# First unit in halves, scalings one head ahead, and the mixer's norm factor on its products

## The reference

```python
h = h + recurrent_block(rmsnorm(h, a_norm), ...)   # u = x @ w_in; conv; gates; scan; @ w_out
h = h + sqrelu_mlp(rmsnorm(h, mlp_norm[0]), w_up[0], w_down[0])
k, v = shared_kv(h, ...)
h = h + chunk_band_attention(rmsnorm(q), k, v, rel_bias) @ b_w_o      # 16 heads
h = h + sqrelu_mlp(rmsnorm(h, mlp_norm[1]), w_up[1], w_down[1])
# second block, on the same h and on mem (256 x 1024)
p = rmsnorm(h, norm_mix_pre) @ w_in_2      # q,k,v of 3 attentions and 3 gates, 5888 columns
h = h + rmsnorm((sum over b of sigmoid(gate_b) * (attention_b @ w_branch_b)) @ w_out_2, ...)
h = h + rmsnorm((gelu(conv(u_gate)) * conv(u_val)) @ w_ffn_down_2, ...)   # conv over tokens
```

## Time and profile before

| | |
|---|---|
| profiled execution, its own time | 1075.28 us |
| its span, first to last instruction | 1073.5 us |
| median of the three timed runs | 1074.75 us |
| PE busy | 1032.0 us, 96% of the span |
| DVE, ACT, POOL busy | 662.0, 556.9, 85.8 us |
| mean granted TensorE clock | 0.990 |
| from HBM | 178.48 MB |

### The profile page before, as it was taken

The page is one execution under the profiler, slowest core; times in us unless marked ns, Lnnn a source line. Parts: engine busy times, 40 slices in busy tenths (PEclk is TensorE's granted clock), DMA queues, the critical chain, the costliest instruction groups (busy, mean ns, idle before and its releaser), DMA issues. The chain is left out here.

```text
span 1073.5 us, 16449 instructions
## 1 busy us (share of the span) xinstructions
PE 1032.0 (96%) x6698; PEld 927.5 (86%) x6698; DVE 662.0 (62%) x950; ACT 556.9 (52%) x817; POOL 85.8 (8%) x109
## 2 busy tenths in 40 slices
PE   5989999999999989999999989999999989999997
PEld 5888899999987755798999979988899879999997
DVE  5769665555557665565555554455655658878775
ACT  6598454444446464454444454455644446655552
POOL 3510010000002210030000000000001600000000
PEclk9989999999999999999999989999999999999999
DMA  9545586555536331475555537543333534655531
GB/s 312 189 137 164 189 302 208 178 184 185 196 118 218 135 118 40 158 238 193 192 186 171 193 101 214 169 146 102 98 137 137 198 117 160 232 170 185 195 118 40
DMA packets 120307, 180.41 MB, mean 168 GB/s; under 512 B 3145, under 2 KB 93609, under 8 KB 120249
## 3 DMA queue, kind: packets, MB, share of 16 engines
q1 hardware_dynamic: 118435, 174.16, 49.3%
q0 software_dynamic: 1696, 5.39, 1.5%
q10 hardware_dynamic: 118, 0.05, 0.0%
HBM read 178.48 MB, written 1.10 MB: 167 GB/s over the span
## 5 line engine op out<-in xcount | busy, mean ns | idle before, releaser
L1037 PE MATMUL PS<-XA,whi 128*128 128x256 f32 x2544 | 468.0, 286 | 4.6 <-DVE XA L1610 3.2
L1559 DVE TENSOR_TENSOR wlo<-raw,whi 128x2048 fp32r<-128x2048 f32 x155 | 356.6, 2305 | 172.3 <-ACT whi L611 172.3
L1037 PEld LDWEIGHTS PS<-XA,whi 128*128 128x128 f32 x2544 | 402.9, 193 | 14.2 <-issue 10.6
L611 ACT ACTIVATE whi<-raw 128x2048 fp32r<-128x2048 f32 x155 | 295.7, 1910 | 138.6 <-PE PS L1082 103.6
L1037 PE MATMUL PS<-XA,wlo 128*128 128x256 f32 x1272 | 361.7, 284 | 0.0
L1037 PEld LDWEIGHTS PS<-XA,wlo 128*128 128x128 f32 x1272 | 245.9, 193 | 0.0
L1082 PE MATMUL PS<-whi,XB 128*128 128x512 f32 x736 | 209.0, 391 | 0.0
L1082 PEld LDWEIGHTS PS<-whi,XB 128*128 128x128 f32 x736 | 135.6, 188 | 26.6 <-issue 0.5
L1082 PE MATMUL PS<-wlo,XB 128*128 128x512 f32 x368 | 117.5, 390 | 0.0
L1082 PEld LDWEIGHTS PS<-wlo,XB 128*128 128x128 f32 x368 | 69.1, 188 | 14.6
L787 ACT ACTIVATE arena<-PS 128x256 f32<-128x256 f32 x64 | 24.2, 383 | 96.2 <-PE PS L1037 95.7
(11 more groups left out here) (221 smaller groups left out, 1108.7 us busy)
## 6 DMA issues: line engine op xcount, KB each, us to landing
raw<-in_w_up SPq DMA_DIRECT2D x32, 1024.0 KB, 5.4
raw<-in_w_down SPq DMA_DIRECT2D x32, 1024.0 KB, 5.0
raw<-in_w_ffn_up SPq DMA_DIRECT2D x22, 1024.0 KB, 5.0
raw<-in_w_in SPq DMA_DIRECT2D x21, 1024.0 KB, 5.2
raw<-in_w_ffn_down SPq DMA_DIRECT2D x11, 1024.0 KB, 4.9
raw<-in_a_w_in SPq DMA_DIRECT2D x8, 1024.0 KB, 8.3
raw<-in_w_kv SPq DMA_DIRECT2D x8, 1024.0 KB, 5.0
raw<-in_w_mem_kv SPq DMA_DIRECT2D x4, 1024.0 KB, 5.1
```

The lines of the kernel that those rows point to most:

```text
L611: act.activation(whi[:, s, :], raw[:, s, :], ACT.Copy).then_inc(s_hi, 1)
L1037: ins = pe.matmul(PS[:, bank_of(g), 0:T], w[:, k, P * m:P * m + P], X[:, k0 + k, part, :], start=(i == 0 and part == 0 and w is hi), stop= ...
L1559: dve.tensor_tensor(wlo[:, s, :], raw[:, s, :], whi[:, s, :].bitcast(F32), ALU.subtract).then_inc(s_lo, 1)
```

## The change

- **Start.** `res` is loaded in two token halves and unit 0 in two halves of k. The 18 loads of small vectors are issued by SP (7) and ACT (11) instead of POOL (5), SP (7) and ACT (6). PE first runs 18 products of `ident` with itself, and 4 more behind the transposes (`keep_warm`). The vector rows are transposed between the two token halves. ACT copies the gains; the other vectors are copied by DVE later. Unit 0 is multiplied with k outermost. Its split is made in two halves on ACT and DVE, the second half on DVE behind four of the `XA` parts. Unit 1 is split on ACT in two halves among the `XA` copies.
- **Recurrent part.** ACT's wait for `s_ew` moves from behind `conv_hi(0)` to ahead of `gate_out(0)`.
- **Sixteen heads.** DVE scales the probabilities of H + 1 where it scaled those of H, behind the row maxima of H + 2; its split halves come one head later. ACT takes the exponentials of H + 2 ahead of the split half. The last split is at head 13 instead of 14.
- **Mixer's norm.** The second MLP's last product is lifted. `first_up` multiplies unit `U_QKV`. Squares are taken behind the `XA` copies, POOL's roots go to `dsc`. In the middle of unit `U_QKV + 1` PE multiplies `dsc` into a row (2 products, bank 7), and ACT copies it to `rstd_row`.
- **Mixer.** DVE evacuates 17 groups with a multiplication by `rstd_row`, followed by its split of unit u + 3; the two value results are scaled by `dsc`. In `gates` DVE multiplies each of the 24 groups by `rstd_row` into SBUF, behind its split; ACT's tanh reads that and stands behind `probs_out`.

The core of the diff:

```diff
@@ ACT, start and recurrent part
-            squares(SQ_NORM[0], res, lambda i: act.wait_ge(s_x, 16))
-            split(0)
-            norm_hi(0, [(XA, R_ANORM)])
-            split(1)
+            squares(SQ_NORM[0], res, lambda i: act.wait_ge(s_x[i // 2], 16))
+            for h, done in enumerate((s_hi0, s_hi)):
+                act.wait_ge(s_landed[0] if h else s_w0, 16)
+                at = slice(UNIT // 2 * h, UNIT // 2 * h + UNIT // 2)
+                act.activation(whi[:, 0, at], raw[:, 0, at], ACT.Copy).then_inc(done, 1)
...
             conv_hi(0)
 
-            act.wait_ge(s_ew, 32)
             rec_unit(2)
...
             conv_hi(3)
+
+            act.wait_ge(s_ew, 32)
             gate_out(0)
@@ DVE, start
+            for h, (ready, done) in enumerate(((s_hi0, s_lo0), (s_hi, s_lo))):
+                dve.wait_ge(ready, 1)
+                at = slice(UNIT // 2 * h, UNIT // 2 * h + UNIT // 2)
+                dve.tensor_tensor(wlo[:, 0, at], raw[:, 0, at], whi[:, 0, at].bitcast(F32), ALU.subtract).then_inc(done, 1)
...
+                for k in range(4 * h, 4 * h + 4):
+                    dve.wait_ge(s_xhi, NORM_HI[0] + k + 1)
...
@@ DVE, sixteen heads
             row_max(1)
+            norm_probs(0)
             for H in range(16):
-                norm_probs(H)
                 if H + 2 < 16:
                     row_max(H + 2)
+                if H + 1 < 16:
+                    norm_probs(H + 1)
...
                 for part in range(2):
-                    if H - part in SPLIT_AT:
-                        split(SPLIT_AT[H - part] + LEAD, part=part)
+                    if H - 1 - part in SPLIT_AT:
+                        split(SPLIT_AT[H - 1 - part] + LEAD, part=part)
@@ PE, mixer's norm
-            norm_T(5)
-            for i in range(2):
-                unit_a(U_QKV + i, G_QMB + 2 * i, xready=NORM_HI[5] if i == 0 else None)
+            first_up(U_QKV, G_QMB, 5, lambda: res_T(1, A_MLP1, 4))
+            have(U_QKV + 1)
+            group(G_QMB + 2, (U_QKV + 1) % SLOTS, 0, W8, KT, XA)
+            pe.wait_ge(s_rstd, ROOTS[SQ_NORM[5]] + TT)
+            for t in range(TT):
+                ins = pe.matmul(PS[:, 7, P * t:P * t + P], dsc[:, DS_MIX + t:DS_MIX + t + 1].to_broadcast([P, P]),
+                                ident[:], start=(t == 0), stop=(t == 1), skip_group_check=True)
+            ins.then_inc(s_bc, 1)
+            group(G_QMB + 3, (U_QKV + 1) % SLOTS, 1, W8, KT, XA)
@@ DVE, mixer
+            def rows_out(u, g, dsts, scale=1.0):
+
+                for m, dst in enumerate(dsts):
+                    dve.wait_ge(s_step, BEFORE(u) + m + 1)
+                    dve.scalar_tensor_tensor(dst, PS[:, bank_of(g + m), 0:T], scale, rstd_row[:], ALU.mult, ALU.mult)\
+                       .then_inc(s_evac, 1)
+                if u > U_QKV:
+                    split(u + LEAD)
...
                 if k % 2 == 0:
                     split(U_G2[b] + k // 2 + LEAD)
+                dve.wait_ge(s_step, BEFORE(U_G2[b]) + k + 1)
+                dve.tensor_tensor(g_br[b][:, k, :], PS[:, bank_of(G_G2[b] + k), 0:T], rstd_row[:], ALU.mult)\
+                   .then_inc(s_evac, 1)
@@ ACT, mixer
-                evac(G_G2[b] + k, BEFORE(U_G2[b]) + k + 1, g_br[b][:, k, :], ACT.Tanh, 0.5)
                 if H <= last:
                     probs_out(H)
+                act.wait_ge(s_evac, G_G2[b] + k + 1)
+                act.activation(g_br[b][:, k, :], g_br[b][:, k, :], ACT.Tanh, scale=0.5).then_inc(s_tanh, 1)
```

More of the change, by code:

```diff
@@ L298, in bass_blocks @@
         s_ident = sem("identity")
[L299 to L300 removed]
+        s_small, s_tables = sem("small_loads"), sem("bias_table_loads")
+        s_x = [sem(f"x_loaded{t}") for t in range(TT)]
+        s_w0 = sem("first_unit_half_landed")
+        s_hi0, s_lo0, s_gain = sem("first_unit_half_hi"), sem("first_unit_half_lo"), sem("norm_gains")
         s_mem = sem("mem_loaded")
@@ L446, in load @@
                 dst = raw[:, slot, :].rearrange("p (k n) -> p k n", k=w_units[u].shape[1])
+                if u == 0:
+                    for h in range(2):
+                        sp.dma_start(dst[:, 4 * h:4 * h + 4, :], w_units[u][:, 4 * h:4 * h + 4, :])\
+                          .then_inc(s_landed[slot] if h else s_w0, 16)
+                    return
                 if u in U_SWQ:
@@ L915, in _ @@
             mlp(1)
-            norm(5, res, [(XA, R_MIX)], added(A_MLP1))
-            two = lambda v, i: [v[:, 2 * i + m, :] for m in range(2)]
-            for i in range(2):
-                unit_a(U_QKV + i, G_QMB + 2 * i, two(qT_mb, i), scale=0.125)
-            for i in range(2):
-                unit_a(U_QKV + 2 + i, G_KMB + 2 * i, two(kT_mb, i))
-            for i in range(2):
-                unit_b(U_QKV + 4 + i)
-            for i in range(2):
-                unit_a(U_QKV + 6 + i, G_QSW + 2 * i, two(qT_sw, i), scale=0.125)
-            unit_a(U_QKV + 8, G_KSW, [kT_sw])
-            for i in range(2):
-                unit_a(U_QKV + 9 + i, G_QME + 2 * i, two(qT_me, i), scale=float(P) ** -0.5)
+            lift_hi(5, [(XA, R_MIX)], U_MLP1 + MLP_UNITS - 1)
+            squares_res(SQ_NORM[5])
+            unit_b(U_QKV)
+            unit_b(U_QKV + 1)
+            act.wait_ge(s_bc, 1)
+            act.activation(rstd_row[:], PS[:, 7, 0:T], ACT.Copy).then_inc(s_row, 1)
+            for i in range(2, 11):
+                unit_b(U_QKV + i)
             def gates(b, k, H, last):
@@ L1881, in _ @@
             mlp(1)
-            dve.wait_ge(s_rstd, ROOTS[SQ_NORM[4]] + TT)
-            add_out(A_MLP1, U_MLP1 + MLP_UNITS - 1, DS_MLP1)
-            norm(5, res, [(XA, R_MIX)], late=U_MLP1 + MLP_UNITS - 1 + LEAD)
-            for i in range(6):
-                split(U_QKV + i + LEAD)
-            dve.wait_ge(s_step, AFTER[U_QKV + 5])
-            dve.tensor_copy(v_mb, PS[:, 6:8, :]).then_inc(s_bev, 1)
-            for i in range(6, 9):
-                split(U_QKV + i + LEAD)
-            dve.wait_ge(s_step, AFTER[U_QKV + 8])
@@ L1894, in _ @@
-            dve.tensor_copy(v_sw, PS[:, 5, 0:T].rearrange("p (t n) -> p t n", t=TT)).then_inc(s_bev, 1)
-            for i in range(9, 11):
-                split(U_QKV + i + LEAD)
+            add_lift(A_MLP1, U_MLP1 + MLP_UNITS - 1, 5, [(XA, R_MIX)], U_MLP1 + MLP_UNITS - 1 + LEAD, DS_MLP1)
+            def rows_out(u, g, dsts, scale=1.0):
[5 more added lines that the diff above has]
+                    split(u + LEAD)
@@ new lines, in _ @@
+            two = lambda v, i: [v[:, 2 * i + m, :] for m in range(2)]
+            split(U_QKV + LEAD)
+            dve.wait_ge(s_row, 1)
+            for i in range(2):
+                rows_out(U_QKV + i, G_QMB + 2 * i, two(qT_mb, i), 0.125)
+            for i in range(2):
+                rows_out(U_QKV + 2 + i, G_KMB + 2 * i, two(kT_mb, i))
+            for i in range(2):
+                split(U_QKV + 4 + i + LEAD)
+            dve.wait_ge(s_step, AFTER[U_QKV + 5])
+            for t in range(TT):
+                ins = dve.tensor_scalar(v_mb[:, t, :], PS[:, 6 + t, :], dsc[:, DS_MIX + t:DS_MIX + t + 1], None, ALU.mult)
@@ new lines, in _ @@
+            ins.then_inc(s_bev, 1)
+            for i in range(2):
+                rows_out(U_QKV + 6 + i, G_QSW + 2 * i, two(qT_sw, i), 0.125)
+            rows_out(U_QKV + 8, G_KSW, [kT_sw])
+            dve.wait_ge(s_step, AFTER[U_QKV + 8])
+            for t in range(TT):
+                ins = dve.tensor_scalar(v_sw[:, t, :], PS[:, 5, P * t:P * t + P], dsc[:, DS_MIX + t:DS_MIX + t + 1], None,
+                                        ALU.mult)
+            ins.then_inc(s_bev, 1)
+            for i in range(2):
+                rows_out(U_QKV + 9 + i, G_QME + 2 * i, two(qT_me, i), float(P) ** -0.5)
```

112 lines of the change are left out of this document (71 added, 41 removed).

## The result

The changed kernel takes 1057.8 us (median of 4 runs, 1055.43 to 1059.32), the kernel before 1074.89 (4 runs, 1071.1 to 1075.15). The ratio is 0.9847, 95% interval 0.9816 to 0.9878: 1.5% less, 16.4 us (13.1 to 19.8). The forecast was 1060.6 with a range of 1054 to 1068.5.

The account below looks back on a forecast made before the run. PE, busy 1032.0 of 1073.5 us, was taken as the bound, so only its waits and low clock could be won. Gains of 5.2 + 4.4 + 5.1 = 14.7 off 1075.3 gave 1060.6 us, range 1054 to 1068.5.

Parts of the forecast that it names:

- Start and recurrent part: 0 to 62 us: moving ACT's wait removes DVE's 6.38 us hole, start 1.2 late; gain 5.2, ends 2.5 and 8.5.
- first scaled copy: Start, on ACT: put at 14.4 us (estimate; 13 to 16) instead of 14.57.
- Their use is small too, since PE waits on DVE in unit 0: Start: the warming products on PE cost nothing and bring little, as PE waits for DVE in unit 0.
- split of unit 3: Start, on DVE: 12.9 us behind the first scaled copy instead of 11.5, so at 27.3, 1.2 late.
- PE's 4.00 us: Recurrent part: wait ahead of the second four gate heads, until 56.54; start forecast at 51.4 without DVE's 6.38 us hole.
- Sixteen heads: 366 to 441 us: scaling one head ahead removes most of 5.1 us of waits for probabilities; gain 4.4, ends 2 and 7.
- Mixer: Norm ahead of the mixer, 628 to 643 us: lifted form wins 6.8 us, broadcast costs 0.4.
- head 16: First head of the mixer: DVE's later split of unit `U_QKV` + 13 delays the row maximum; cost 1.3 us.
- second rival: Gates: DVE late with its products, 12 splits of 2.29 us paid in full, 27 us, so 1088; chance 0.03.
- first rival: Gate heads and head 6: the clock holds, saving 1.6, 1.7 and 1 us, so 1056.3; chance 0.22.
- third rival: Start: later split, late weights and ACT's wait at its new place eat the 5.2 us, so 1065.8; chance 0.2.
- The fourth: Rival: two of the three stretches are given back at the next wait, so 1070.3; chance 0.07.

Follow-up runs that it names:

- start_and_wait: The kernel before with the new start and the moved wait for `bias_rows` together, nothing else: 1068.81 us, ratio 0.9934.
- gaps_filled: The changed kernel with products of no use in three waits of PE, at the second four gate heads and ahead of the FFN: 1055.45 us, ratio 0.9818.
- start_only: The kernel before with the new start alone, the wait for `bias_rows` left where it was: 1074.97 us, ratio 0.9999.

## Why the prediction was right, and where its terms were off

**Start and recurrent part: forecast 5.2, measured 8.25.** The mechanism is right: the wait for `bias_rows` was the largest row (6.1 us alone), and the gate heads start at 49.50 where the prediction had 51.4. The mis-sized term is the first scaled copy: 14.4 forecast, 13.06 measured. The step that failed is "Their use is small too, since PE waits on DVE in unit 0" (of the warming products). The eight transposes of each token half stand ahead of ACT's copy, and at the high clock they take 1.10 instead of 1.94 us; without the warming the copy comes at 14.62, close to the forecast. From the copy to the split of unit 3 it was 12.43, not 12.9. From there to the gate heads it was 24.0, as forecast (51.4 - 27.3 = 24.1). The last 1.2 us, from 7.04 at the gate heads to 8.25 at 93 us, come from the low clock: all 24 products of these heads ran at it before (55 to 63 us), only some of them after (51 to 55). Keeping the clock high there altogether would have brought nothing more: start_and_wait had no low clock on these heads, led by 9.4 us at 66 and, behind the wait for ACT at 73 us, by the same 8.2. The forecast had no term for that wait. One reading was wrong without harm: the prediction let PE's 4.00 us hang on DVE. They hung on ACT's sigmoids, which stand behind the same convolution of DVE and so moved with it. The lead was not given back up to 360 us, as the prediction held; but the start alone gave nothing that could be measured, since it ended at the wait where that was.

**Sixteen heads: forecast 4.4, measured 3.8 in the trace, 5.1 alone.** The waits for probabilities went to nothing (0.7 forecast). Not foreseen: a wait of 0.5 us for the scaled keys, because PE comes there 1.3 us earlier while DVE scales them (383.07 to 384.29) behind the low part of head 3, for which it stood 2.00 us itself, until ACT's high part was there (382.73); and the low clock lasted twice as long in this execution as in the one before. PE was idle for 4.2 us less over these heads (3.7 instead of 7.9), and its instructions took 0.4 more.

**Mixer: forecast 6.4 with its broadcast, measured 6.3; head 16 forecast -1.3, measured -1.2.** Both by their mechanism: the earlier split takes the 1.1 us back. DVE's products with `rstd_row` took 421 ns each (24 of them) and 424 (17), against the 420 of the earlier trace rows:

```profile
L1980 DVE TENSOR_TENSOR arena<-PS,rstd_row 128x256 f32<-128x256 f32 x24 | 10.1, 421 | 10.3 <-PE PS L1053 10.3
```

Both wait for PE (10.3 and 20.8 us). Of the 17, one is waited for: 0.5 us for the queries ahead of the first scores, where PE waited 0.5 for ACT's copy before. No wait of PE for the 24 is in the trace, so the gates cost 0, as forecast, and the second rival (DVE late there) is out.

**The low clock: not in the sum.** 1.1 us were lost at the FFN, where nothing was changed: the low clock lasted from 860 to 867 us after and from 878 to 882 before. PE is idle for the same 3.85 us around it in both, and of the eleven executions without the filling seven had the shorter low clock there and four the longer, so its length is a chance of the execution. The prediction treated the low clock as a fixed cost of each place, with a rival in which it vanishes. Neither holds: at one place with one wait it is sometimes there and sometimes not, and its length differs. The first rival (the clock holds at the gate heads and head 6) didn't come true in the profiled execution, where both places had it. The four runs of the changed kernel differ by it: two with a mean granted clock of 0.995 took 1055.43 and 1056.53, near the 1056.3 of this rival, and two with 0.991 and 0.992 took 1059.32 and 1059.07; where it was low in those without a profile isn't known. At the gate heads the rival would not have been worth its 1.6 us, since filling that gap won 0.2 in all.

**The sum.** 5.2 + 4.4 + 5.1 = 14.7 forecast; 8.25 + 3.78 + 6.30 - 1.19 = 17.1 measured, less 1.1 at the FFN. So the total of 14.7 for 16.0 hides a start that gave 3 us more than its term and a loss at the FFN that had none; that they offset each other in part is luck. The third rival (the start gives nothing back) is what the start alone did, but not with the wait moved. The fourth, two stretches given back, is out.

Of the signs named beforehand: no ACT wait for `bias_rows`, heads near 51 (49.5), at most 1 us of waits for scaled probabilities (none), about 7.5 us from the last MLP product to the end of the first unit at a clock of 1.00 (617.21 to 624.08, 6.9, and 0.8 of transposes now inside the MLP), 1.3 us at head 16 (0.77 idle, 1.2 by the rows of both). None of the signs against it appeared.

## What to carry to other kernels

A wait that stands in an engine's list far ahead of the work that needs it can cost most of its length there, and swallows what is won ahead of it: the new start was worth 0.8 us at the gate heads until the wait was moved, too little to be measured in the times, and 2.0 after. The engine that a profile names for a wait is a guess: ask in the code which semaphore the waiting instruction needs. And where PE must idle for 2 us or more, it is worth trying a few products of no use to keep the clock for what follows. Follow the lead to the next wait: it gave 2.5 us ahead of the FFN, where what follows hangs on PE, and 0.2 at the gate heads, where a copy of ACT 20 us later took back the rest.

## What was not expected of the hardware

The low clock behind an idle stretch is not the same from one execution to the next: the wait of 2.0 to 2.2 us at head 6 brought it in eight of eleven profiled executions, for 4 to 8 us, and cost 3.5 us of PE's time in the changed kernel. In the profiled executions of the two kernels with products of no use in the gaps the clock stayed high in both places; ahead of the FFN it was low in all eleven others. The recorded granted clock doesn't tell of the start: it reads 1.00 for 0 to 10 us, while the 18 products of the warming (36 instructions) took 6.74 us, and without them the transposes at 10 us ran at the low rate (1.94 us for eight, against 1.10). The Trainium skill, TensorE: Matmul & The Clock Gate, part 1, says of a kernel's start that the number of slow matmuls differs from run to run of the same kernel; the traces agree: of the 35 distances from one warming instruction to the next, between 16 (gaps_filled) and 28 (start_only) are over 0.16 us in the eight kernels that have them, and the rest 0.11 to 0.16. The table of low stretches shows such a difference for waits in the middle of a kernel too.
